# Probability-value products of an attention stage: FP32 against F32R in high and low parts

## The chip, the cores and the metric

The kernel runs on one core of a Trainium2 chip. The metric is the device time of one execution in microseconds, lower is better. The times shown are the median of the runs named; the profile is one further execution.

## The reference

A two-layer trunk over 512 latent tokens of width 1024, with 256 context tokens. Layer 0 mixes with a gated DeltaNet (4 heads) and, beside it, grouped attention; layer 1 mixes with a short convolution; both have a gated MLP. The change touches the attention alone:

```python
def gqa_softmax(q, k, v):
    # q: (B, Tq, 8 heads, 64); k, v: (B, S, 2 heads, 64)
    qg = q.reshape(b, tq, ATT_KV_HEADS, ATT_GROUPS, ATT_HD)
    s = jnp.einsum('bqkgd,bskd->bkgqs', qg, k) * (ATT_HD ** -0.5)
    p = jax.nn.softmax(s, axis=-1)
    o = jnp.einsum('bkgqs,bskd->bqkgd', p, v)
```

Queries are the 512 latent tokens, keys and values all 768 tokens. Everything is FP32.

## The kernel before, in words

All tensors lie with features or tokens over the 128 partitions. The heavy products (input and output projections, MLP) hold every operand as an F32R high part and a low part (the value less its high part) and make three F32R products of each pair: high by high, high by low, low by high. ScalarE writes high parts of weights (`split_hi`, line 1386), VectorE low parts (`split_lo`, line 1781). Each engine has its own program, written out in order; semaphores tie them, and an engine that waits holds up all that stands behind in its program.

The attention follows the DeltaNet. Two query heads, one for each key head, are worked as a pair p (4 pairs), one in partitions 0 to 63 and one in 64 to 127. A pair has 6 key tiles n of 128 keys; g = 6 p + n counts 24 items. Three things are done:

- Row maxima of a pair: `row_fill` (line 946, TensorE) makes scores of 128 queries by 384 keys for both heads into banks 2 and 3, and `row_max` (line 2080, VectorE) reduces each bank. The next `row_fill` waits for that reduction, as there is one pair of banks. A pair needs 8 of these. The first pair's stand before item 0; those of pair p + 1 are done in items n = 0 to 3 of pair p, two an item, so 12 of the 24 items have them. `row_peak` joins them and POOL writes them as a diagonal (`peak_diag`, line 2612), which a product with ones takes off the scores.
- Scores, keys over partitions: `scores_turned(g)` (line 970) makes eight matmuls into two banks, 0 and 1 or 4 and 5 by turns. It waits for the exponential of item g - 2 (semaphore `pexp`). ScalarE takes the exponential of the 128x1024 scores into `prob` (line 1588).
- Values: `values(g, half)` (line 990) multiplies `V1[half]` (64 columns of values, 64 of ones, so that the sums come along) by the probabilities of one head, in FP32, and adds over n in banks 6 and 7. It is issued two items behind the scores (`VALUE_LAG`), first half between the two row fills, second half behind them.

The TensorE loop (line 1107) has also columns of the modulation vectors (`mod_part`), `head_sums` in items 12 to 15 (each waits for a square that ScalarE issues at the end of its item), `sums_turned` and `inverse_rows` at n = 4 and 5, and `head_rows` in items 18 to 21. In item 16 the columns wait for a square root (`osd`, line 1629).

ScalarE's loop (line 1615) has, per item, the exponential, half of a modulation product (`mod_products`, four scalings of 128x256, items 0 to 21), and at some items `heads_out` (four copies that free banks 6 and 7; items 7, 13, 19), `head_hi` (12, 18), squares (11 to 14) and high parts of DeltaNet heads (19 to 22). POOL adds up each modulation product in three additions (line 2486) after every second item. VectorE's loop (line 2252) has the row maxima, `inverse_sums` and `heads_normed` at n = 4 and 5, `gated` (18 to 21) and `gated_lo` (20 to 23). When the last `gated_lo` is done (`mix0`), ScalarE makes the high part of the first weights of the output projection (line 1635), VectorE the low part, and `out_units` (line 1210) begins.

V comes in as `av`, is turned by TensorE (`value_turns`), and copied by ScalarE from PSUM into `V1` (line 1579), beside the last DeltaNet step. VectorE then makes the last six row-maximum pairs of pair 0 (line 2213).

## Time and profile before

| | us |
|---|---|
| median of 3 runs | 1664.26 (1662.99 to 1668.65) |
| the profiled execution | 1658.18 |
| its span, first to last instruction | 1656.4 |
| TensorE busy | 1550.1 (94%) |
| VectorE busy | 838.1 (51%) |
| ScalarE busy | 648.6 (39%) |
| POOL busy | 306.0 (18%) |

The profiled execution was 6 us faster than the median of the runs, and 5 faster than the fastest; its durations are used against its own time. Matmuls overlap, so the distance from one start to the next says more than a duration. PEclk is the granted TensorE clock as a share of 2.4 GHz; 0.50 is 1.2 GHz.

### The profile page before, as it was taken

Reading aid. Unit: us, or ns where it says so; the run is one execution under the profiler, and the core shown is the slowest. Engines: PE = TensorE matmul, PEld = TensorE weight load, DVE = VectorE, ACT = ScalarE, POOL = GpSimd, SP = SyncE. Lnnn points to the kernel's source line nnn. Section 1 sums busy time; section 2 is a strip of 40 time slices with the busy share of each in tenths; the row PEclk is TensorE's granted clock in tenths of the full one; section 3 lists DMA queues with packets and bytes.
Section 4 is the critical chain, followed back from the end, with each engine's and each line's share of the span. In section 5 each row is a group of like instructions: output and inputs, shape, how many; then the busy total and the mean of one; then the engine's idle time right before and its main releaser. Section 6 shows DMA issues by size and latency. Waiting matters only on the chain.

```text
span 1656.4 us, 19507 instructions
## 1 busy us (share of the span) xinstructions
PE 1550.1 (94%) x7832; PEld 1251.0 (76%) x7832; DVE 838.1 (51%) x1119; ACT 648.6 (39%) x990; POOL 306.0 (18%) x218
## 2 busy tenths in 40 slices
PE   8899896689979999899999999899998999999997
PEld 2688686578964557688888888778886888888886
DVE  2645523886553237755544343566667544444222
ACT  2443446301225564255533222256542434443221
POOL 3028602334644443000000011000021000000000
PEclk9999899679989999999999999899999999999999
DMA  9325601000021215134423222255522233222221
GB/s 349 102 89 175 181 26 39 1 1 1 1 77 62 92 51 153 51 118 137 131 96 101 92 93 96 93 163 184 170 86 67 76 102 101 83 95 96 92 93 51
DMA packets 153908, 160.19 MB, mean 97 GB/s; under 512 B 11383, under 2 KB 151144, under 8 KB 152808
## 3 DMA queue, kind: packets, MB, share of 16 engines
q1 hardware_dynamic: 153344, 158.95, 29.9%
q8 instruction: 53, 0.87, 0.2%
q10 hardware_dynamic: 488, 0.18, 0.0%
q14 instruction: 23, 0.19, 0.0%
HBM read 157.03 MB, written 2.10 MB: 96 GB/s over the span
## 4 chain that ended last, share of the span: by engine, by line
PE 82%; DVE 10%; ACT 2%; POOL 2%; issue 2%; DMA 0%; SPq 0%; DVEq 0%; ACTq 0%; POOLq 0%
PE ps L600 19%; PE ps L602 19%; PE ps L601 19%; PE ps L998 2%; PE ps L960 2%; DVE sub_prod L1996 1%; DVE blocks_inv L1999 1%; PE ps L985 1%; PE ps L1148 1%; PE ps L658 1%; PE ps L1150 1%; PE ps L1149 1%; DVE w_lo L1781 1%; PE ps L1170 1%; DVE att_top L2085 1%
## 5 line engine op out<-in xcount | busy, mean ns | idle before, releaser
L1781 DVE TENSOR_TENSOR w_lo<-w_raw,w_hi 128x2048 fp32r<-128x2048 f32 x100 | 234.2, 2342 | 454.0 <-ACT w_hi L1386 454.0
L600 PE MATMUL ps<-h_hi,w_hi 128*128 128x512 f32 x968 | 378.5, 391 | 2.0 <-DVE w_lo L1781 2.0
L601 PE MATMUL ps<-h_lo,w_hi 128*128 128x512 f32 x968 | 377.5, 390 | 0.0
L602 PE MATMUL ps<-h_hi,w_lo 128*128 128x512 f32 x968 | 377.4, 390 | 0.0
L1386 ACT ACTIVATE w_hi<-w_raw 128x2048 fp32r<-128x2048 f32 x100 | 191.3, 1913 | 258.9 <-PE ps L602 222.4
L600 PEld LDWEIGHTS ps<-h_hi,w_hi 128*128 128x128 f32 x968 | 182.2, 188 | 40.2 <-DVE w_lo L1781 2.6
L602 PEld LDWEIGHTS ps<-h_hi,w_lo 128*128 128x128 f32 x968 | 182.2, 188 | 38.1
L601 PEld LDWEIGHTS ps<-h_lo,w_hi 128*128 128x128 f32 x968 | 182.3, 188 | 37.6
L2635 POOL TENSOR_TENSOR sum_acc_y<-sum_acc_y,sum_y 128x512 f32<-128x512 f32 x18 | 25.7, 1427 | 584.1 <-ACT sum_y L1655 584.1
L600 PE MATMUL ps<-mid_hi,w_hi 128*128 128x512 f32 x338 | 133.0, 394 | 0.0
L602 PE MATMUL ps<-mid_hi,w_lo 128*128 128x512 f32 x338 | 131.8, 390 | 0.0
L601 PE MATMUL ps<-mid_lo,w_hi 128*128 128x512 f32 x338 | 131.5, 389 | 0.0
L2635 POOL TENSOR_TENSOR tmp<-tmp,tmp 128x512 f32<-128x512 f32 x6 | 7.8, 1295 | 379.1 <-ACT tmp L1651 379.1
L602 PEld LDWEIGHTS ps<-mid_hi,w_lo 128*128 128x128 f32 x338 | 63.4, 188 | 13.4
L601 PEld LDWEIGHTS ps<-mid_lo,w_hi 128*128 128x128 f32 x338 | 63.5, 188 | 12.9
L600 PEld LDWEIGHTS ps<-mid_hi,w_hi 128*128 128x128 f32 x338 | 63.5, 188 | 12.8
L2486 POOL TENSOR_TENSOR mod_raw_e<-mod_raw_e 128x1024 f32<-128x1024 f32 (+1 forms) x24 | 57.4, 2392 | 84.6 <-ACT mod_raw_e L1440 83.7
L2085 DVE TENSOR_REDUCE att_top<-ps 128x1 f32<-128x384 f32 x64 | 32.7, 552 | 58.3 <-PE ps L960 58.1
L2486 POOL TENSOR_TENSOR mod_raw_c<-mod_raw_c 128x1024 f32<-128x1024 f32 (+2 forms) x33 | 49.1, 1487 | 44.3 <-ACT mod_raw_c L1597 42.6
L2288 DVE TENSOR_SCALAR y<-ps,post_w 128x512 f32<-128x512 f32 x32 | 23.9, 748 | 63.8 <-ACT tmp L1651 30.3
L1703 ACT ACTIVATE mid_hi<-tmp 128x512 f32 (+1 forms) x44 | 27.1, 633 | 66.4 <-DVE tmp L2392 66.4
L998 PE MATMUL ps<-prob,V 128*128 128x512 f32 x96 | 52.7, 647 | 0.1
(374 smaller groups left out, 2611.3 us busy)
## 6 DMA issues: line engine op xcount, KB each, us to landing
w_raw<-in_ffn_w_up SPq DMA_DIRECT2D x44, 1024.0 KB, 5.1
w_raw<-in_ffn_w_down SPq DMA_DIRECT2D x16, 896.0 KB, 4.8
mod_raw_e<-in_mod_w SPq DMA_DIRECT2D x12, 1024.0 KB, 5.3
w_raw<-in_sc_w_in SPq DMA_DIRECT2D x12, 1024.0 KB, 5.3
mod_raw_c<-in_mod_w SPq DMA_DIRECT2D x11, 1024.0 KB, 5.2
mod_raw_s<-in_mod_w SPq DMA_DIRECT2D x11, 1024.0 KB, 7.9
w_raw<-in_hyb_w_in SPq DMA_DIRECT2D x9, 1024.0 KB, 7.9
mod_raw_a<-in_mod_w SPq DMA_DIRECT2D x8, 1024.0 KB, 16.1
```

Source lines behind the costliest of these rows:

```text
L600: mm(dst, hi, xh[:, k0 + k, :], start=first and k == 0, stop=False)
L601: mm(dst, hi, xl[:, k0 + k, :], start=False, stop=False)
L602: i = mm(dst, lo, xh[:, k0 + k, :], start=False, stop=last and k == nk - 1)
L960: m = mm(bank(2 + half, 384), q[r, p, qs], k[r, ks], start=i == 0, stop=i == 2)
L998: mm(bank(6 + half), V1[half][:, n, :], prob[g % 4][:, half * SEQ:(half + 1) * SEQ], start=n == 0, stop=n == NT - 1).then_inc(sem("pv"), 1)
L1386: nc.scalar.activation(whi[s][:, :], raw[s][:, :], ACT.Copy).then_inc(sem("w_hi"), 1)
L1703: nc.scalar.activation(mid_hi[:, bass.ds(2 * i + (2 * j0 + r), 1), :].rearrange("p c t -> p (c t)"), tmp[2 * par + r][:, :], ACT.Copy).the ...
L1781: V.tensor_tensor(wlo[s][:, :], raw[s][:, :], f32(whi[s][:, :]), ALU.subtract).then_inc(sem("w_lo"), 1)
L2085: V.tensor_reduce(top[:, c:c + 1], bank(2 + half, 384), AX.X, ALU.max).then_inc(sem("mx"), 1)
L2288: V.tensor_scalar(y[:, t, :], b, pw, None, ALU.mult).then_inc(sem("yev"), 1)
L2486: G.tensor_tensor(dst, a, b, ALU.add).then_inc(sem("mod_acc"), 1)
L2635: G.tensor_tensor(a[:, :], a[:, :], q[t % 2][:, :], ALU.add).then_inc(sem("ya"), 1)
```

## The change

`V1` and `prob` become F32R high parts (`Vh`, `PTh`) and low parts (`Vl`, `PTl`). ScalarE takes the exponential of an item twice, once into the F32R high part and once in FP32 into one of two `prob` buffers (now where `tmp` lies); VectorE subtracts the first from the second (`probability_lo`), one item behind, between the two `row_max` of an item. `values` makes three F32R products for one FP32 product and waits for the low part. `scores_turned` waits for both exponentials. Ahead of the loop VectorE writes the low part of V, in front of six pairs of row maxima, and POOL sets the other halves.

```diff
@@ -178,9 +178,12 @@
         peak = region("att_peak", 2 * 8, 107.125)
         isum = region("att_isum", 8, 107.1875)
         one_r = region("one_r", P, 107.5, F32R)
-        prob = [region(f"prob{i}", 2 * SEQ, 62 + 4 * i) for i in range(4)]
+        PTh = [region(f"PTh{i}", 2 * SEQ, 62 + 4 * i, F32R) for i in range(4)]
+        PTl = [region(f"PTl{i}", 2 * SEQ, a0, F32R) for i, a0 in enumerate((78, 82, 108, 112))]
+        prob = [place(f"prob{i}", 2 * SEQ, F32, tmp_at + 4 * K * i) for i in range(2)]
         diag = [region(f"peak_diag{i}", 2 * SEQ, 40 + 4 * i, F32R) for i in range(2)]
-        V1 = [view(region(f"V1{i}", NT * P, 116 + 3 * i), "p (n t) -> p n t", t=P) for i in range(2)]
+        Vh = [view(region(f"Vh{i}", NT * P, a0, F32R), "p (n t) -> p n t", t=P) for i, a0 in enumerate((116, 122))]
+        Vl = [view(region(f"Vl{i}", NT * P, a0, F32R), "p (n t) -> p n t", t=P) for i, a0 in enumerate((119, 54))]
         att_o = region("att_o", SEQ, 48)
         att_s = region("att_s", SEQ, 50)
         att_n = region("att_n", SEQ, 52)
@@ -972,11 +975,11 @@
                 p, n = divmod(g, NT)
                 b = 4 * (g % 2)
                 if g == 0:
-                    pe.wait_ge(sem("V"), 3)
+                    pe.wait_ge(sem("V"), 5)
                     pe.wait_ge(sem("oe"), 8)
                     pe.wait_ge(sem("vset"), 1)
                 if g >= 2:
-                    pe.wait_ge(sem("pexp"), g - 1)
+                    pe.wait_ge(sem("pexp"), 2 * (g - 1))
                 if n == 0:
                     pe.wait_ge(sem("dg"), p + 1)
                 ks = slice(n * P, (n + 1) * P)
@@ -990,13 +993,15 @@
             def values(g, half):
 
                 p, n = divmod(g, NT)
-                pe.wait_ge(sem("pexp"), g + 1)
+                pe.wait_ge(sem("PT"), g + 1)
                 if g == 0:
-                    pe.wait_ge(sem("vset"), 3)
+                    pe.wait_ge(sem("vset"), 5)
                 if n == 0 and p:
                     pe.wait_ge(sem("ov"), 4 * (p - 1) + 2 * half + 2)
-                mm(bank(6 + half), V1[half][:, n, :], prob[g % 4][:, half * SEQ:(half + 1) * SEQ], start=n == 0,
-                   stop=n == NT - 1).then_inc(sem("pv"), 1)
+                b, cols = bank(6 + half), slice(half * SEQ, (half + 1) * SEQ)
+                mm(b, Vh[half][:, n, :], PTh[g % 4][:, cols], start=n == 0, stop=False)
+                mm(b, Vh[half][:, n, :], PTl[g % 4][:, cols], start=False, stop=False)
+                mm(b, Vl[half][:, n, :], PTh[g % 4][:, cols], start=False, stop=n == NT - 1).then_inc(sem("pv"), 1)
 
             def sums_turned(p):
 
@@ -1218,7 +1223,7 @@
                         if j:
                             pe.wait_ge(sem("scb"), KC - 2)
                         else:
-                            pe.wait_ge(sem("pexp"), NITEM)
+                            pe.wait_ge(sem("pexp"), 2 * NITEM)
                         for k in range(KC):
                             if j == 0 and k == 3:
                                 sums_turned(3)
@@ -1576,7 +1581,7 @@
             act.wait_ge(sem("V"), 1)
             act.wait_ge(sem("rp"), 2 * NT)
             for half, r in enumerate(HALF):
-                nc.scalar.activation(V1[half][:, :, r], bank(0, ALL).rearrange("p (n t) -> p n t", t=P)[:, :, r],
+                nc.scalar.activation(Vh[half][:, :, r], bank(0, ALL).rearrange("p (n t) -> p n t", t=P)[:, :, r],
                                      ACT.Copy).then_inc(sem("V"), 1)
             act.wait_ge(sem("oe"), 8)
 
@@ -1585,8 +1590,11 @@
                 act.wait_ge(sem("st"), g + 1)
                 if g >= 4:
                     act.wait_ge(sem("pv"), 2 * (g - 3))
-                nc.scalar.activation(prob[g % 4][:, :], bank(4 * (g % 2), 2 * SEQ), ACT.Exp,
-                                     scale=HD ** -0.5).then_inc(sem("pexp"), 1)
+                b = bank(4 * (g % 2), 2 * SEQ)
+                nc.scalar.activation(PTh[g % 4][:, :], b, ACT.Exp, scale=HD ** -0.5).then_inc(sem("pexp"), 1)
+                if g >= 2:
+                    act.wait_ge(sem("PT"), g - 1)
+                nc.scalar.activation(prob[g % 2][:, :], b, ACT.Exp, scale=HD ** -0.5).then_inc(sem("pexp"), 1)
 
             def mod_products(j, half):
 
@@ -2210,10 +2218,22 @@
                     dve.wait_ge(sem("mod_done"), 2 * SC0)
                 V.tensor_tensor(sums_tile(j), t[:, 0, :], t[:, 1, :], ALU.add).then_inc(sem("late"), 1)
 
+            dve.wait_ge(sem("Sp"), 2 * NT - 2)
+            for half, r in enumerate(HALF):
+                dve.wait_ge(sem("V"), 3)
+                V.tensor_tensor(Vl[half][:, :, r], bank(0, ALL).rearrange("p (n t) -> p n t", t=P)[:, :, r],
+                                f32(Vh[half])[:, :, r], ALU.subtract).then_inc(sem("V"), 1)
             for j in range(2, NL):
                 for f in range(2):
                     row_max(0, j, f)
             row_peak(0)
+
+            def probability_lo(g):
+
+                dve.wait_ge(sem("pexp"), 2 * (g + 1))
+                if g >= 4:
+                    dve.wait_ge(sem("pv"), 2 * (g - 3))
+                V.tensor_tensor(PTl[g % 4][:, :], prob[g % 2][:, :], f32(PTh[g % 4][:, :]), ALU.subtract).then_inc(sem("PT"), 1)
 
             def inverse_sums(p):
 
@@ -2254,6 +2274,8 @@
                 fills = p + 1 < NPAIR and n < 4
                 if fills:
                     row_max(p + 1, n, 0)
+                if g:
+                    probability_lo(g - 1)
                 if g in (12, 18):
                     heads_lo(p - 2)
                 if fills:
@@ -2271,6 +2293,7 @@
                     gated(g - 18)
                 if 20 <= g:
                     gated_lo(g - 20)
+            probability_lo(NITEM - 1)
             dve.wait_ge(sem("mod_done"), 2 * (ATT0 + 8))
             split_lo(U_WOUT, 0)
             heads_lo(2)
@@ -2607,7 +2630,8 @@
             pool.wait_ge(sem("Sp"), 2 * NT - 2)
             for half in range(2):
                 r = HALF[1 - half]
-                G.memset(V1[half][:, :, r], 1.0).then_inc(sem("vset"), 1)
+                G.memset(f32(Vh[half])[:, :, r], 1.0).then_inc(sem("vset"), 1)
+                G.memset(f32(Vl[half])[:, :, r], 0.0).then_inc(sem("vset"), 1)
 
             def peak_diag(p):
 
```

## Rows read from the trace of the kernel before

**Rows 1.** Page, part 1: busy us, share of the span, instructions.

```profile
PE 1550.1 (94%) x7832; PEld 1251.0 (76%) x7832; DVE 838.1 (51%) x1119; ACT 648.6 (39%) x990; POOL 306.0 (18%) x218
```

**Rows 2.** Page, part 4: chain of waits, shares of the span by line.

```profile
PE ps L600 19%; PE ps L602 19%; PE ps L601 19%; PE ps L998 2%; PE ps L960 2%; DVE sub_prod L1996 1%; DVE blocks_inv L1999 1%; PE ps L985 1%; PE ps L1148 1%; PE ps L658 1%; PE ps L1150 1%; PE ps L1149 1%; DVE w_lo L1781 1%; PE ps L1170 1%; DVE att_top L2085 1%
```

**Rows 3.** Windows: us, busy of PE, PEld, DVE, ACT, POOL; PEclk, DMA, GB/s.

```profile
505.00:520.00 15.00, 14.69 (x65) 6.97 (x62) 4.25 (x9) 8.43 (x17) 8.24 (x7) 1.00 0.17 52
...
580.00:595.00 15.00, 12.02 (x51) 7.03 (x52) 1.08 (x4) 7.00 (x13) 5.42 (x4) 0.77 0.21 70
```

**Rows 4.** Timeline of PE, items 3 to 5: start, us, [idle before, releaser].

```profile
510.46 1.13 PE L998 MATMUL ps<-prob,V 128*128 128x512 f32 x2
511.74 0.44 PE L960 MATMUL ps<-ak_hi,aq_hi 64*128 64x384 f32 x2 [0.16 <-DVE att_top L2085]
...
517.25 0.50 PE L985 MATMUL ps<-aq_hi,ak_hi 64*128 64x512 f32 x2
...
518.72 1.88 PE L998 MATMUL ps<-prob,V 128*128 128x512 f32 x4
520.52 0.50 PE L985 MATMUL ps<-aq_hi,ak_hi 64*128 64x512 f32 x2
```

**Rows 5.** Timeline of ACT, item 4.

```profile
515.20 1.02 ACT L1588 ACTIVATE prob<-ps 128x1024 f32<-128x1024 f32 x1 [2.74 <-PE ps L987]
516.12 1.69 ACT L1597 ACTIVATE mod_raw_c<-mod_raw_c,cvec 128x256 f32<-128x256 f32 x4
```

**Rows 6.** Timeline of PE, output projection, first and last of 31 starts.

```profile
638.00 0.39 PE L600 MATMUL ps<-mix_hi,w_hi 128*128 128x512 f32 x1
...
644.80 0.39 PE L600 MATMUL ps<-mix_hi,w_hi 128*128 128x512 f32 x1
```

**Rows 7.** Timeline of PE, item 14.

```profile
565.70 1.02 PE L1031 MATMUL ps<-const,o_square 128*128 128x1 f32 x8 [0.35 <-ACT o_square L1625]
```

**Rows 8.** Timeline of PE and ACT, item 16.

```profile
581.31 1.28 ACT L1629 ACT_TABLE_LOAD   x1
...
582.98 0.56 PE L620 MATMUL ps<-const,mod_raw_c 128*128 128x1 f32 x2 [4.32 <-issue]
...
583.39 2.05 PE L998 MATMUL ps<-prob,V 128*128 128x512 f32 x2
...
585.24 0.42 PE L620 MATMUL ps<-const,mod_raw_c 128*128 128x1 f32 x2
```

**Rows 9.** Timeline ahead of item 0: ACT, DVE, POOL.

```profile
477.06 0.85 ACT L1579 ACTIVATE V<-ps 128x384 f32<-128x384 f32 x2
...
480.99 0.69 DVE L2061 TENSOR_TENSOR oT<-oT,ps 128x512 f32<-128x512 f32 x1 [1.15 <-PE ps L927]
...
489.01 1.90 POOL L2620 TENSOR_TENSOR peak_diag<-const,att_peak 128x1024 fp32r<-128x1024 f32 x1 [6.98 <-DVE att_peak L2093]
```

**Rows 10.** Groups of VectorE instructions: busy us, mean ns, idle before.

```profile
L2085 DVE TENSOR_REDUCE att_top<-ps 128x1 f32<-128x384 f32 x50 | 25.5, 552 | 54.3 <-PE ps L960 54.2
...
L2205 DVE TENSOR_TENSOR mod_raw_f<-mod_raw_f 128x1024 f32<-128x1024 f32 x6 | 7.3, 1214 | 0.0
```

**Rows 11.** Timeline of POOL and DVE, item 20.

```profile
601.60 4.86 POOL L2486 TENSOR_TENSOR mod_raw_c<-mod_raw_c 128x1024 f32<-128x1024 f32 x3 [3.92 <-ACT mod_raw_c L1597]
...
601.85 2.67 DVE L2244 TENSOR_TENSOR oT<-oT,gT 128x512 f32<-128x512 f32 x1
```

**Rows 12.** Timeline of PE and ACT, item 18 to the output projection.

```profile
593.09 0.50 PE L985 MATMUL ps<-aq_hi,ak_hi 64*128 64x512 f32 x2
...
618.95 1.91 ACT L1386 ACTIVATE w_hi<-w_raw 128x2048 fp32r<-128x2048 f32 x1 [3.05 <-DVE mix_lo L2249]
...
623.30 0.50 PE L1231 MATMUL ps<-mix_hi,w_hi 128*128 128x512 f32 x1 [1.65 <-DVE w_lo L1781]
```

**Rows 13.** Windows of PE: us, PE busy, PEclk, DMA, GB/s.

```profile
486.00:489.00 3.00, 1.07 (x6) 0.66 0.87 276
...
621.00:624.00 3.00, 1.35 (x5) 1.00 0.28 75
```

## The prediction

> **What bounds the kernel now.** I read the page first: TensorE is busy 94% of the span, VectorE 51%, ScalarE 39% [rows 1]. In the chain of waits the weight products (lines 600 to 602) hold over half; the probability-value product, line 998, the line to be changed, holds 2% [rows 2]. So what can move lies in the attention stage, from about 491 to 623 us. The windows show TensorE full there (14.8 of 15 us) and ScalarE at little more than half; only 580 to 595 has a hole and a low granted clock [rows 3].
>
> Then the TensorE timeline of single items. There are 24 items g (head pair p, key tile n). In an item without row maxima, line 998 takes 518.72 to 520.52, 1.80 us for two FP32 products (two records each), and the pitch is 3.27 us. In an item with row maxima (12 of them, 10 with values) each half of the values stands alone, and the second row product waits for VectorE's two reductions of the first: the values after 510.46 end before that wait (0.16 us) does [rows 4].
>
> ScalarE takes 0.92 us from one start to the next for the exponential and 1.60 for four scalings (1.70 less the same overlap of 0.1), 2.52 an item [rows 5].
>
> **TensorE.** 48 FP32 products become 144 F32R ones. F32R products of this shape in the output projection start 31 times in 6.80 us, 0.227 apart [rows 6]. Three are 0.68 against 0.86 for one FP32 product (1.80 less 0.08 for the change of tile shape, halved): 0.17 saved per half, 0.35 per item, 8.3 us over 24 items if all of it shows. It doesn't:
> - Items 2, 3, 6 to 9, 12, 14, 15: the first half's saving falls into the wait for VectorE [rows 4]; 9 x 0.17 = 1.5.
> - Items 4, 5, 10: all, 3 x 0.35 = 1.0. ScalarE's new 3.44 us is above their pitch, but they come in pairs after items with slack (ScalarE was idle for 2.74 us before item 4's exponential [rows 5]) and TensorE runs two items ahead.
> - Item 11 leads to head_sums, which wait for a square that ScalarE issues behind exponentials and scalings. One more exponential (0.92) eats the slack: 0. Item 13: head_sums already waited 0.35 for that square [rows 7]. There ScalarE's waits for values go and the exponential comes, and the square is ready when it was: 0.
> - Item 17: 0.35.
> Together -2.9.
>
> **Item 16.** TensorE stands 4.32 us while ScalarE does exponential, scalings, a table load and a square root [rows 8]. The second exponential lies in that chain: +0.92. The item's values then run at the low clock ([rows 3]: a mean of 0.77 over 15 us is 1.2 GHz for 6.9 of them), where one FP32 product and its column took 1.85 [rows 8]; three F32R products at twice 0.227 are 1.36, so about 0.35 of its 1.72 is saved per half, 0.7. Net +0.2.
>
> **The start.** V's low part is two VectorE subtractions of 128x384 from PSUM, behind the last oT addition (481.68) and ahead of the row maxima on which the first diagonal, and so all items, wait [rows 9]. Nearest rows: 0.69 for 128x512 from PSUM, 0.55 for a 128x384 reduction [rows 9, 10]. I take 0.52 each, +1.1 (bounds 0.9 and 1.4). V's high copies are done by 477.9 and hide. POOL's extra memsets hide in its 6.98 us of idle time before the diagonal [rows 9]. No DMA is added; SP's loads of modulation weights follow the columns, which stay behind their additions as now.
>
> **VectorE's low part.** 24 subtractions of 128x1024 in SBUF. The same shape elsewhere takes 1.21 us [rows 10]. In an item with maxima it stands between the two pairs of reductions: from the end of the first row product 0.1 + 1.0 + 1.2 + 1.0 = 3.4 us (with issue), and the next row product is due after 1.3 + 0.7 + 0.8 + 1.6 = 4.4. It costs nothing while that 1 us of cover holds; values run two items late, so they don't wait.
> But two-input VectorE work in SBUF does wait for POOL. At 601.85 a 128x512 product took 2.67 us instead of 0.69, until POOL's 128x1024 addition from 601.60 was over [rows 11]. POOL adds after every second item. In the maxima items its last, shortest addition meets the subtraction: up to 0.9 us late, just covered. Should it be the longest (2.3), 1.4 us would show, in three items (7 to 8 and the like): bound +4, I take 0.
>
> **The last six items** (18 to 23, no maxima). I drew up a schedule from 593.09 (t = 0) with the durations above, queue by queue. ScalarE: 1.84 + 1.60 for items 18 to 21, 1.84 for the others, 2.2 for heads_out, 0.5 for each of five high parts, first start at 1.7, end near 24.0. That alone would hold the loop some 1 us longer than now. VectorE: item 18's gated ends at 8.0, the low part of item 18 at 9.2, gated(1) waits for POOL's first addition until 12.1, the low part of item 19 for the second until 14.6; TensorE needs it at 12.9. The low part of item 21 lands at 23.6 (wanted at 21.6), so inverse_rows(2), heads_normed(2) and gated_lo(3) end at 28.9; w_hi, which waits for the last of them, now starts at 25.9. Behind it stand w_hi (1.9) and w_lo (the rest of the 4.35 us to the projection), then the output projection: 33.2 against 30.2 [rows 12]. So this stretch, instead of giving 6 x 0.35 = 2.1, costs +3.0. Bounds: +1 if VectorE always gets in ahead of POOL (ScalarE alone), +5 if every low part meets an addition.
>
> **Sum:** -2.9 + 0.2 + 1.1 + 3.0 = **+1.4 us**. The profiled execution took 1658.18 (span 1656.4) and would become 1659.6. The median of the runs shown is 6 us above it, so the forecast is 1664.3 + 1.4 = **1665.7**. Elsewhere nothing changes: the probability buffers move to free places, F32R outputs cost ScalarE no more (w_hi's 128x2048 takes 1.91 [rows 12]).
>
> **Rivals.**
> *A. The clock falls (slower).* In the schedule TensorE waits 1.8 us in item 21, 2 in item 23, 1.5 in the two value rounds behind it and 2 before the output projection. In this trace the granted clock fell between 486 and 489, where TensorE waited for row maxima and was busy 1.07 of 3 us; yet from 621 to 624 it was busy 1.35 of 3 and kept 1.00 [rows 13]. It decides if the waits from item 21 on are as dense as those ahead of 487. The Trainium skill, TensorE: Matmul & The Clock Gate, HAM oscillation, says that matmul bursts with waits between keep losing the full clock; by that rule this change, which puts waits between short bursts, would lose it here, while the rows speak both ways. Price: the low stretch of item 16 lasted 6.9 us [rows 3]; once or twice that at 1.2 GHz costs the output projection 3.5 to 7. With the +1.4 and the upper bound of the late stretch: +5 to +10, 1669 to 1674. Chance 0.2.
> *B. Everything is covered (faster).* VectorE beats POOL, ScalarE's idle time absorbs the exponentials (it works 8.4 of 15 us [rows 3]), and the last items give their 2.1. Then -2.9 - 2.1 + 0.2 + 1.1 = -3.7, 1660.6; with the whole 8.3 saved and the start free it is -8.3 + 0.9 = -7.4, 1657. For it: the average idle. Against: the last items' queues. Chance 0.12 for somewhere under 1662, 0.06 for over 0.3%.
> *C. The maxima items become bound by VectorE.* Up to 1.4 us in three items, and a little in others: +4 on top, 1669 to 1670. Chance 0.1.
> *D. It saves TensorE nothing.* If the three products came 0.29 us apart they would take the 0.86 of the FP32 one: 0 + 0.9 + 1.1 + 3.0 = +5.0, 1669.3. Against it: the 31 starts of the same shape and type [rows 6]. Chance 0.02.
>
> **Numbers.** Forecast 0.56, within 1662 to 1669. A change under 0.3% (5 us) can't be told from none. Slower by more: most of A and a little of C, 0.18. Faster: 0.06. Same: 0.76. The range takes in B's partial case below and A's above: 1659.5 to 1672.
>
> **What would show it.** Line 998's successors 0.227 us apart in threes; the first row product after them waiting about 0.3 instead of 0.16; the two VectorE subtractions before the third pair of reductions, diagonal 1 us later; the hole at item 16 at 5.2 us; low parts of 1.2 us, some of 2 to 3.5 where POOL adds; TensorE waiting in items 21 and 23 for them; w_hi of the output projection issued some 3 us later after the start of item 18. Wrong if the maxima items lengthen (then C), if the last six items shrink (B), or if the granted clock in the output projection is below 1 (A).

## The result, and the profile after

The changed kernel took 1673.59 us (median of 6 runs, 1670.40 to 1683.72), the kernel before 1667.47 in the same comparison (6 runs, 1662.99 to 1672.90): ratio 1.0066, interval 1.0043 to 1.0088. A second comparison, ten runs of the changed kernel beside 33 of before, gave 1.0062 (1.0036 to 1.0088). The medians alone are 6.1 us apart in the first comparison and 11.8 in the second (1678.04 against 1666.21). So it is slower by some 10 us; the forecast of no change was wrong, and 1673.59 is above the range. Of the 7.9 us between it and the forecast of 1665.7, 3.2 are the kernel before itself, whose median was 1664.26 when the forecast was made and 1667.47 here.

The profiled execution took 1672.36 (span 1670.6), 14.2 more than that of before. The page's part 1 for the kernel after:

```profile
PE 1557.5 (93%) x7880; PEld 1270.1 (76%) x7880; DVE 870.8 (52%) x1145; ACT 669.3 (40%) x1014; POOL 315.6 (19%) x220
```

TensorE is busy 7.4 us more than in [rows 1], though its products were to take 8.3 less. I cut both traces at landmarks: the end of the last oT addition, and the starts of the first score product of some items (line 985 before, 988 after). In us:

| stretch | before | after | difference | predicted |
|---|---|---|---|---|
| start to the last oT addition | 481.68 | 485.51 | +3.8 | 0 |
| to item 0 | 9.37 | 11.33 | +1.96 | +1.1 |
| items 0, 1 | 11.87 | 12.66 | +0.79 | 0 |
| items 2 to 15 | 74.11 | 79.22 | +5.11 | -2.5 |
| item 16 | 11.33 | 11.39 | +0.06 | +0.2 |
| item 17 | 4.73 | 4.02 | -0.71 | -0.35 |
| item 18 to the output projection | 30.21 | 31.85 | +1.64 | +3.0 |
| projection to the end | 1033.10 | 1034.62 | +1.5 | 0 |

The first and last rows hold code that the change does not touch; the clock that an execution happens to get moves them, which I call its draw: between 250 and 480 us the windows add up to 68 us below full clock here and 58 before, and 58 again in the second profiled execution of the changed kernel (its start takes 482.04). That leaves 8.9 us between the last oT addition and the projection, where I had +1.4, and 5.11 of it where I had a gain.

The reason stands in the windows of TensorE in items 6, 14 and 23 of the kernel after (columns: us, PE busy, PEclk, DMA share, GB/s):

```profile
528.00:531.00 3.00, 2.10 (x14) 1.00 0.00 0
531.00:534.00 3.00, 2.78 (x13) 0.67 0.18 44
534.00:537.00 3.00, 3.00 (x10) 0.50 0.91 306
...
573.00:576.00 3.00, 2.54 (x17) 1.00 0.00 0
576.00:579.00 3.00, 3.00 (x14) 0.57 0.02 5
...
633.00:636.00 3.00, 1.45 (x7) 1.00 0.08 15
```

A PEclk of 0.50 is 1.2 GHz. The clock fell twice amid busy work, at about 532 and 576, and came back some seven us later each time; in the kernel before it is 1.00 from 501 to 582. Products at 1.2 GHz take nearly twice as long (timeline, item 6): their starts are 0.42 apart, where they are 0.23 apart at 2.4 GHz.

```profile
533.97 0.63 PE L1003 MATMUL ps<-PTl,Vh 128*128 128x512 f32 x1
534.39 0.63 PE L1004 MATMUL ps<-PTh,Vl 128*128 128x512 f32 x1
```

Between 480 and 660 us the windows of the kernel after add up to 44.4 us at 1.2 GHz, before to 20.5. The difference is the two stretches in the items and a longer one at the start: 23.9 us, from 487.7 to 511.6, against 13.7 before. The longer one reaches 2.1 us into item 2, which takes 6.00 where the second profiled execution has 5.12; so 0.9 of the +5.11 comes from the start and not from the items' own waits. In the last window, where Rival A looked for the fall, TensorE waits half of the time and keeps 1.00.

What TensorE does ahead of such a fall, item 3 of the kernel after (timeline):

```profile
517.77 0.50 PE L1002 MATMUL ps<-PTh,Vh 128*128 128x512 f32 x1
518.11 0.39 PE L1003 MATMUL ps<-PTl,Vh 128*128 128x512 f32 x1
518.34 0.40 PE L1004 MATMUL ps<-PTh,Vl 128*128 128x512 f32 x1
519.05 0.45 PE L963 MATMUL ps<-ak_hi,aq_hi 64*128 64x384 f32 x2 [0.32 <-DVE att_top L2093]
```

Here the three products are 0.23 apart, as forecast, and the wait behind them is 0.32 instead of 0.16 [rows 4], as forecast too. Item 6 has a longer one (timelines of POOL, VectorE and TensorE, kernel after):

```profile
521.25 2.81 POOL L2644 TENSOR_TENSOR peak_diag<-const,att_peak 128x1024 fp32r<-128x1024 f32 x1 [7.14 <-DVE att_peak L2101]
...
524.03 10.79 POOL L2509 TENSOR_TENSOR mod_raw_c<-mod_raw_c 128x1024 f32<-128x1024 f32 x6
...
524.33 3.18 DVE L2236 TENSOR_TENSOR PTl<-prob,PTh 128x1024 fp32r<-128x1024 f32 x1 [2.02 <-ACT prob L1597]
...
529.60 0.35 PE L623 MATMUL ps<-const,mod_raw_c 128*128 128x1 f32 x2 [0.90 <-POOL mod_raw_c L2509]
```

POOL's diagonal takes 2.81 instead of 1.90 [rows 9], its additions run late, VectorE's low part takes 3.18 instead of 1.21 [rows 10], and the column product of item 6 waits 0.90 us for POOL. VectorE and POOL delay each other.

### The profile page after: what moved, and what is told of

Its sections match the earlier page's. It is cut to its first block, busy times and chain, and to the rows that moved or that the text cites. A ratio compares the mean times of both kernels' runs of the same rounds, so it can differ in the third digit from the quotient of the medians.

```text
span 1670.6 us, 19676 instructions
## 1 busy us (share of the span) xinstructions
PE 1557.5 (93%) x7880; PEld 1270.1 (76%) x7880; DVE 870.8 (52%) x1145; ACT 669.3 (40%) x1014; POOL 315.6 (19%) x220
## 4 chain that ended last, share of the span: by engine, by line
PE 77%; DVE 11%; POOL 4%; ACT 4%; issue 3%; DMA 0%; SPq 0%; DVEq 0%; ACTq 0%; POOLq 0%
PE ps L603 18%; PE ps L605 18%; PE ps L604 18%; POOL mod_raw_e L2509 2%; PE ps L963 2%; DVE blocks_inv L2007 2%; DVE sub_prod L2004 1%; PE ps L1153 1%; PE ps L661 1%; DVE w_lo L1789 1%; PE ps L1154 1%; PE ps L1155 1%; PE ps L1175 1%; PE ps L988 1%; PE ps L719 1%
## 5 line engine op out<-in xcount | busy, mean ns | idle before, releaser
L603 PEld LDWEIGHTS ps<-mid_hi,w_hi 128*128 128x128 f32 x338 | 63.9, 189 | 12.7
L2509 POOL TENSOR_TENSOR mod_raw_c<-mod_raw_c 128x1024 f32<-128x1024 f32 (+2 forms) x33 | 54.9, 1663 | 42.9 <-ACT mod_raw_c L1605 41.1
L1704 ACT ACTIVATE tmp<-tmp 128x512 f32<-128x512 f32 x44 | 27.8, 633 | 62.8 <-DVE tmp L2397 62.2
```

The source lines that it names most:

```text
L603: mm(dst, hi, xh[:, k0 + k, :], start=first and k == 0, stop=False)
L1704: nc.scalar.activation(tmp[2 * par + r][:, :], tmp[2 * par + r][:, :], ACT.Silu).then_inc(sem("sg"), 1)
L2509: G.tensor_tensor(dst, a, b, ALU.add).then_inc(sem("mod_acc"), 1)
```

## Experiments

Two theories after the result. Theory C: the shorter products leave TensorE more waiting in the maxima items, and the clock falls there. Theory Q: the added work in the queues of ScalarE, VectorE and POOL costs the time. A third is that the low clock at the start carries over into the items.

**No low part at all.** One exponential, no subtraction; the second product reads PTh, so three F32R products remain.

```diff
-                pe.wait_ge(sem("PT"), g + 1)
+                pe.wait_ge(sem("pexp"), 2 * (g + 1))
...
-                mm(b, Vh[half][:, n, :], PTl[g % 4][:, cols], start=False, stop=False)
+                mm(b, Vh[half][:, n, :], PTh[g % 4][:, cols], start=False, stop=False)
...
-                nc.scalar.activation(PTh[g % 4][:, :], b, ACT.Exp, scale=HD ** -0.5).then_inc(sem("pexp"), 1)
-                if g >= 2:
-                    act.wait_ge(sem("PT"), g - 1)
-                nc.scalar.activation(prob[g % 2][:, :], b, ACT.Exp, scale=HD ** -0.5).then_inc(sem("pexp"), 1)
+                nc.scalar.activation(PTh[g % 4][:, :], b, ACT.Exp, scale=HD ** -0.5).then_inc(sem("pexp"), 2)
...
-                if g:
-                    probability_lo(g - 1)
...
-            probability_lo(NITEM - 1)
```

> The changed kernel without the second exponential and without VectorE's low part of the probabilities; the second of the three F32R products takes the high part again, so TensorE does the same work and the low part of the probabilities is left out of the result. Theory Q (the loss comes from the queues: ScalarE's second exponential, VectorE's subtraction and its waits for POOL): all of it goes, TensorE saves its 0.35 us an item where no row maxima bind, and the kernel comes out 3 to 6 us under the kernel before, a ratio of 0.997. Theory C (the loss is granted clock: two extra stretches at 1.2 GHz in items 6 and 14, because short waits of TensorE follow shorter products): waits for row maxima are still 0.3 us per maxima item, stretches at 1.2 GHz stay between 512 and 588 us, and the time is within 3 us of the kernel before or above it.

Measured: 1663.60 (10 runs), ratio 0.9988 (0.9964 to 1.0013). Items 2 to 15 take 74.71, with low clock in the first 2.0 us of item 2 and from 575 to 582; item 16 takes 10.54 and the last stretch 28.76. From 1.0062 and 1.0066 to 0.9988 is some 12 us: so much hangs on the second exponential and the subtractions, with what they do to the clock. And the F32R products alone bring nothing that can be measured over the whole kernel.

**FP32 product, all the rest kept.** One FP32 product of PTh and Vh, both FP32; both exponentials, all subtractions and their waits stay (the regions `PTh` and `Vh` are declared FP32 too).

```diff
-                mm(b, Vh[half][:, n, :], PTh[g % 4][:, cols], start=n == 0, stop=False)
-                mm(b, Vh[half][:, n, :], PTl[g % 4][:, cols], start=False, stop=False)
-                mm(b, Vl[half][:, n, :], PTh[g % 4][:, cols], start=False, stop=n == NT - 1).then_inc(sem("pv"), 1)
+                mm(b, Vh[half][:, n, :], PTh[g % 4][:, cols], start=n == 0, stop=n == NT - 1).then_inc(sem("pv"), 1)
```

> The changed kernel with all that ScalarE, VectorE and POOL do, but with one FP32 product of the high parts (kept in FP32 here) as in the kernel before: only TensorE's part is undone. The low parts are computed and not used. Theory Q: the queues cost what they cost and TensorE saves nothing, so it is as slow as the changed kernel or up to 3 us slower, 8 to 14 us above the kernel before. Theory C: TensorE's waits in maxima items shrink to those of the kernel before, the granted clock stays at 1.00 from 512 to 588 us, and the kernel is 3 to 6 us above the kernel before: 2 of the start, 3 of the last items, 1 of item 16.

Measured: 1672.43, ratio 1.0037 (1.0014 to 1.0060). The clock stays up in items 2 to 15 (windows of TensorE, the kernel with the FP32 product):

```profile
531.00:534.00 3.00, 2.94 (x16) 1.00 0.04 9
534.00:537.00 3.00, 3.00 (x17) 1.00 1.01 328
...
576.00:579.00 3.00, 2.94 (x14) 1.00 0.07 22
```

They take 75.55, 1.4 more than before. But the low clock of the start reaches 2.2 us into item 2 here as well (6.23 against 5.27), so the queue work itself costs 0.5 in items 3 to 15 (69.32 against 68.85). It costs 0.8 in item 16 (12.15) and 1.7 in the last stretch (31.89). Ahead of item 2 this execution is 2.7 longer, with 23.9 us of low clock at the start against 13.7; how much of that is the queue's was not told apart. So both halves of the cause count: the queue work by itself, and the low clock in the items, which is absent here with the longer product.

**Filler in the maxima items.** One extra 128x512 F32R product of 0.23 us, its result never read, behind the first half of the values in each of the ten maxima items that have values.

```diff
+                if fills and g >= VALUE_LAG:
+                    pe.wait_ge(sem("pexp"), 2 * g)
+                    mm(bank(4 * ((g + 1) % 2)), Vh[0][:, n, :], PTh[(g - VALUE_LAG) % 4][:, 0:SEQ], start=True, stop=True)
```

> The changed kernel with one extra F32R 128x512 product (0.23 us, result overwritten) in each of ten items with row maxima, where TensorE waits 0.31 us for VectorE. Theory C: TensorE is busy through these waits, fewer stretches at 1.2 GHz between 512 and 588 us, 3 to 7 us faster than the changed kernel. Theory Q: the waits for the queues are what they were, the filler is hidden or costs 0.1 an item: same time to 1 us slower.

Measured: 1667.76, ratio 1.0022 (1.0004 to 1.0040). Windows of TensorE in this kernel:

```profile
549.00:552.00 3.00, 2.73 (x27) 1.00 0.07 21
552.00:555.00 3.00, 3.00 (x21) 1.00 0.00 0
555.00:558.00 3.00, 3.00 (x18) 1.00 0.49 137
558.00:561.00 3.00, 3.00 (x20) 1.00 0.61 213
...
570.00:573.00 3.00, 3.00 (x23) 1.00 0.94 315
...
585.00:588.00 3.00, 3.00 (x12) 0.50 0.59 182
```

Items 2 to 15 take 72.97 instead of 79.22, with no low clock until item 16's hole. More work made the items shorter by 6 us, of which 0.9 is item 2, where this execution has no low clock from the start (73.22 to 67.85 for items 3 to 15). TensorE waits for no reduction there any more. The filler is F32R too, so the type of the products alone does not bring the clock down; the gaps between them are what was changed.

**V's low part later**, behind the row maxima and the peak of pair 0.

```diff
             dve.wait_ge(sem("Sp"), 2 * NT - 2)
+            for j in range(2, NL):
+                for f in range(2):
+                    row_max(0, j, f)
+            row_peak(0)
             for half, r in enumerate(HALF):
...
-            for j in range(2, NL):
-                for f in range(2):
-                    row_max(0, j, f)
-            row_peak(0)
```

> The changed kernel with V's low part written by VectorE behind the row peak of pair 0 instead of ahead of the last six pairs of row maxima. Both theories: the 1.0 us leaves the chain to the first scores (11.3 us from the end of the last oT addition in the changed kernel, 9.4 in the kernel before), so 10.3 or less. Theory C adds that the extra low-clock row products ahead of the diagonal go too, 9.4 to 9.6, 2 us in all; theory Q gives 1.0.

Measured: 1667.41, ratio 1.0036 (1.0011 to 1.0062). Item 0 starts 10.20 behind the last oT addition instead of 11.33: the 1.1 is the two subtractions, which the timeline of the changed kernel has as one row:

```profile
485.42 1.01 DVE L2224 TENSOR_TENSOR Vl<-ps,Vh 128x384 fp32r<-128x384 f32 x2
```

In total it can't be told from the changed kernel; its trace too has a low stretch inside the items (531 to 538).

**Second exponential without the subtraction.** As in the first experiment, but ScalarE keeps both exponentials, the second never read and without its wait for PT.

> The changed kernel with ScalarE's second exponential but without VectorE's low part of the probabilities (the second product takes the high part again, the low part is left out of the result). It splits the cost of the last six items, from the first scores of item 18 to the output projection: 31.9 us in the changed kernel, 28.8 without both, 30.2 before. If ScalarE's serial work holds them, 30.5 to 31.9; if VectorE's waits for POOL hold them, 28.8 to 29.5. Item 16 (to the first scores of 17) should stay at 11.4 and be 10.5 only without the exponential. Whole kernel: 0 to 3 us above the kernel before.

Measured: 1663.46, ratio 0.9987 (0.9961 to 1.0013). Last stretch 29.74, between the two answers that I had allowed; items 2 to 15 72.71, with 3.4 us of low clock from 574; item 16 11.39, as expected.

**Subtraction without the second exponential.** PTl is PTh minus PTh, of the same shape.

```diff
-                V.tensor_tensor(PTl[g % 4][:, :], prob[g % 2][:, :], f32(PTh[g % 4][:, :]), ALU.subtract).then_inc(sem("PT"), 1)
+                V.tensor_tensor(PTl[g % 4][:, :], f32(PTh[g % 4][:, :]), f32(PTh[g % 4][:, :]), ALU.subtract).then_inc(sem("PT"), 1)
```

> The changed kernel with VectorE's subtraction of the same size, but of the high part from itself, and without the second exponential (the low part is zero, left out of the result). If VectorE behind POOL holds the last six items, they take 31 to 31.9 us here; if ScalarE does, 28.8 to 29.5. Item 16 takes 10.5. The column product of item 6, for which TensorE waited 0.9 us on POOL's additions, waits here too if VectorE's subtractions are what delays POOL. Whole kernel: 0 to 3 us above the kernel before.

Measured: 1669.13, ratio 1.0017 (0.9991 to 1.0044). Items 2 to 15 take 79.69, with low clock until 511 (5.2 us of item 2) and from 573 to 586; item 16 takes 10.83, with low clock from 590; the last stretch takes 32.96, of which part is 3 us of low clock at 624. The column product of item 6 waits 1.09 us for POOL, as it does with the real subtraction, and 0.23, for VectorE, without any: so the subtractions are what delays POOL. The exponential costs 1 us in the last stretch (28.76 to 29.74) and 0.5 in item 12 (6.40 to 6.90); the subtraction is the expensive one of the two.

**The changed kernel again.**

> The changed kernel again, beside the others on one chip. Theory C (granted clock): it is the slowest of the four, 7 to 12 us above the kernel before, and its profile has at least one stretch at 1.2 GHz between 512 and 588 us. If the first comparison owed its size to where the clock happened to fall, 4 to 7 us. Theory Q has no reason for a change from run to run.

Measured: 1678.04 (10 runs, 1670.21 to 1683.33), ratio 1.0062 (1.0036 to 1.0088). Its profiled execution has one long stretch at 1.2 GHz in place of two short ones (windows of TensorE):

```profile
552.00:555.00 3.00, 2.73 (x20) 1.00 0.00 0
555.00:558.00 3.00, 2.78 (x12) 0.58 0.17 45
558.00:561.00 3.00, 3.00 (x10) 0.50 0.89 304
...
600.00:603.00 3.00, 3.00 (x13) 0.50 0.75 228
603.00:606.00 3.00, 3.00 (x22) 0.95 0.38 127
```

Low from 555 to 603; items 2 to 15 take 85.66, item 16 12.56. The place of the fall differs from one execution to the next; the ten runs lie in two groups, 1670.2 to 1675.6 with a mean clock of 0.947 to 0.950, and 1680.5 to 1683.3 with 0.941 to 0.943. The six runs of the first comparison lie in the same two groups, four and two.

**All gaps filled.** Fillers as above, V's low part later, and the kernel's own `warm` products (line 1104 of the changed kernel) in three places: one before each of pair 0's last four row products, four ahead of item 0, five in item 16's hole. (The text on the kernel before speaks of six such pairs of row maxima; line 1104 and the trace have four.)

```diff
             for j in range(2, NL):
                 for f in range(2):
+                    warm(5, 1)
                     row_fill(0, j, f)
+            warm(5, 4)
...
+                if g == 16:
+                    pe.wait_ge(sem("pexp"), 32)
+                    warm(4, 5)
```

> The changed kernel with filler products in ten maxima items, V's low part behind the first row peak, and filler products (FP32, 0.86 us) between the last row products of pair 0, ahead of the first scores and in the hole of item 16. Theory C: no stretch at 1.2 GHz from 487 to 640 us; against the changed kernel that gives back 5 us in the maxima items, 3 to 4 at the start and 2 behind item 16, so 1 to 4 us under the kernel before. Theory Q: only the 1 us of V's low part, and the fillers cost up to 1: as slow as the changed kernel.

Measured: 1659.93 (12 runs, 1654.68 to 1661.99), ratio 0.9963 (0.9944 to 0.9982). That is 6 us under the kernel before, where 1 to 4 were expected. No low clock between 480 and 660 us. Windows of TensorE from item 6 to item 16:

```profile
519.00:534.00 15.00, 14.33 (x80) 1.00 0.23 72
534.00:549.00 15.00, 14.91 (x90) 1.00 0.44 139
549.00:564.00 15.00, 14.20 (x91) 1.00 0.22 71
564.00:579.00 15.00, 14.91 (x72) 1.00 0.22 71
```

**The kernel before, with the warm products at the start and in item 16 only** (the last edit; the count waited for is 16, since it has one exponential an item).

> The kernel before with the same FP32 fillers between the last row products of pair 0, ahead of the first scores and in the hole of item 16. Theory C: the stretches at 1.2 GHz at 487 and 582 us go, 20 us of low clock in all; the time from the last oT addition to the output projection falls from 141.6 to about 136 (start -1, items 0 and 1 -3.5, item 16 -2), and the kernel is 3 to 6 us under the kernel before, 0 to 3 above or under the changed kernel with all fillers. That says what the change itself is worth with the clock held: near nothing.

Measured: 1658.22 (12 runs, 1653.92 to 1665.33), ratio 0.9952 (0.9930 to 0.9975). That is 8 us under the kernel before, where 3 to 6 were expected. No low clock between 480 and 660 us either, and without a filler in the items. This pair shows the change with the clock held in both: from the last oT addition to the projection 136.57 with the F32R products, 135.79 without, a difference of 0.8. In the first kernel V's low part stands behind the row maxima; where the change has it, it costs 1.1 more, so with the clock held the change would cost about 1.9 (an estimate from these two differences), against the +1.4 of the forecast. Pitch from item to item (from the starts of the first score products):

```
item        2    3    4    5    6    7    8    9   10   11   12   13   14   15
before   5.27 5.34 3.73 3.28 5.67 5.34 5.67 5.35 4.17 4.29 6.57 6.13 7.16 6.13
changed  5.11 5.17 3.40 2.93 6.73 5.18 5.52 5.17 3.82 3.98 6.90 5.98 7.10 5.98
```

**Ends filled, items not.** The kernel with all gaps filled, less the ten fillers.

> The version with all fillers, less the ten of 0.23 us in the maxima items. Theory C: the clock starts full at 490 and falls in some executions and stretches between 512 and 588 us, where the waits of 0.3 us stand again; 3 to 8 us slower than with all fillers, near the kernel before, with runs further apart than those of the version with all fillers (7 us from lowest to highest). If the low clock of those items was only a consequence of the low start, it stays full and the time equals that with all fillers.

Measured: 1671.76 (12 runs, 1659.73 to 1672.62), ratio 1.0011 (0.9986 to 1.0035). The start is as full as in the last two kernels (item 0 at 10.15, items 0 and 1 in 8.33), and yet the clock falls in item 12. Timeline, then windows of TensorE, of this kernel:

```profile
552.66 1.02 PE L1036 MATMUL ps<-const,o_square 128*128 128x1 f32 x8 [0.26 <-ACT o_square L1638]
...
555.74 0.59 PE L623 MATMUL ps<-const,mod_raw_c 128*128 128x1 f32 x2 [0.22 <-DVE att_top L2098]
556.26 0.69 PE L963 MATMUL ps<-ak_hi,aq_hi 64*128 64x384 f32 x2
```

```profile
552.00:555.00 3.00, 2.74 (x20) 1.00 0.00 0
555.00:558.00 3.00, 2.78 (x12) 0.63 0.10 27
558.00:561.00 3.00, 3.00 (x10) 0.50 0.94 322
...
588.00:591.00 3.00, 3.00 (x9) 0.50 0.00 0
```

Two waits of a quarter of a microsecond, then 37.5 us at 1.2 GHz: items 2 to 15 take 85.63 instead of 72.97. The fall is no consequence of the low clock at the start; that rival is out, but for the 0.9 us of item 2. The fall is a matter of chance in part: two of the 12 runs took 1659.7, seven 1671.7 to 1672.6, which is about the 12.7 us that the profile shows. With all fillers none of 12 runs was above 1662.0, and none of ten above 1660.6 in the next version, which was timed on the same chip as this one.

**POOL's late additions cut.** The kernel with all gaps filled, but POOL's additions of the modulation products from 20 on are one column wide; most of that sum is left out.

```diff
-                mod_add(3 * j, slot[:, 0:4, :], slot[:, 0:4, :], slot[:, 4:8, :])
+                w = slice(0, 1) if 20 <= j < LATE else slice(0, UW)
+                mod_add(3 * j, slot[:, 0:4, w], slot[:, 0:4, w], slot[:, 4:8, w])
```

> The version with all fillers, with POOL's additions of the last three modulation products (those behind items 17, 19 and 21) cut to one column of 256; most of that sum is left out of the result. If VectorE's waits for POOL hold the last six items, they take 29.5 to 30.5 us from the first scores of item 18 to the output projection instead of 31.9, and VectorE's subtractions there take 1.2 us each. If the plain length of VectorE's and ScalarE's work holds them, 31.5 to 31.9.

Measured: 1658.29, ratio 0.9951 (0.9932 to 0.9970). Last stretch 29.72 instead of 31.86. The subtractions there, first in the kernel with all gaps filled, then in this one (timelines of VectorE, other rows left out):

```profile
602.96 1.22 DVE L2244 TENSOR_TENSOR PTl<-prob,PTh 128x1024 fp32r<-128x1024 f32 x1
...
606.08 3.42 DVE L2244 TENSOR_TENSOR PTl<-prob,PTh 128x1024 fp32r<-128x1024 f32 x1
...
611.11 1.74 DVE L2244 TENSOR_TENSOR PTl<-prob,PTh 128x1024 fp32r<-128x1024 f32 x1
```

```profile
605.45 1.22 DVE L2244 TENSOR_TENSOR PTl<-prob,PTh 128x1024 fp32r<-128x1024 f32 x1
608.82 1.22 DVE L2244 TENSOR_TENSOR PTl<-prob,PTh 128x1024 fp32r<-128x1024 f32 x1
612.13 1.23 DVE L2244 TENSOR_TENSOR PTl<-prob,PTh 128x1024 fp32r<-128x1024 f32 x1 [0.66 <-ACT prob L1605]
```

So 2.1 us of the last stretch are VectorE's waits for POOL, and the subtractions themselves are hidden there: without them, but with the second exponential, it took the same 29.74.

**All profiled executions together.** Low clock between the first scores of item 3 and of item 16, one execution each:

| version | us at 1.2 GHz |
|---|---|
| FP32 products: before; before with warm products; FP32 product in the changed kernel | 0, 0, 0 |
| F32R products, no fillers in the items: the changed kernel, twice; V's low part later; ends filled | 13.7, 33.8; 6.8; 33.7 |
| the same without subtractions: one exponential; two | 6.8; 3.4 |
| the same with the subtraction, one exponential | 13.0 |
| F32R products, fillers in the items: fillers alone; all gaps filled; POOL's late additions cut | 0, 0, 0 |

All seven with shorter products and open waits have it and none of the six others. The subtractions are not needed for a fall. The sizes are draws, as the two executions of the changed kernel show, and executions that were not profiled can differ.

## Why the prediction was wrong, by its steps

**The step that failed** is in the part on TensorE: "the first half's saving falls into the wait for VectorE; 9 x 0.17". I booked the saved time as a longer wait that costs nothing. The wait came to the size I gave it (0.32), but with such waits the clock of TensorE fell in all seven profiled executions, and at 1.2 GHz the products behind it take nearly twice as long (0.42 us against 0.23). I had set a price on a fall of the clock only behind item 21; in the maxima items it stood at nothing. In place of -2.5 for items 2 to 15 stand +5.1 in one profiled execution and +11.5 in the other (74.11 against 85.66). With the ten waits filled it is -1.1. The link from the waits to the clock rests on filling them: no fall in three profiled executions with the fillers, at least one in each of the seven without. Ten extra products in another place were not tried.

**Rival A** named this mechanism and put it in the wrong place: I looked for the long waits (items 21, 23 and the projection), and those kept the full clock, while short ones in a stretch that I read as "full" lost it. Its span, 1669 to 1674, holds the median by luck: it was worked out from late waits and the late stretch, which is not how the time came. The sign that I gave for Rival C, maxima items that lengthen, came true through the clock too. Behind the rows: the Trainium skill, TensorE: Matmul & The Clock Gate, A second HAM failure mode, describes a kernel in which TensorE idles briefly between groups of matmuls, often enough for the clock to swing. By that rule this would have been the rival to price; the trace agrees with it, with waits of 0.2 to 0.3 us ahead of the fall at 555.7. I had taken the section ahead of it, on longer waits.

**TensorE with the clock held.** The pitches of the two kernels without low clock give 0.15 to 0.18 for items 2, 3, 7, 8, 9 and 15 (forecast 0.17), 0.33 to 0.35 for 4, 5 and 10 (0.35), 0.31 for 11 and 0.15 for 13 (forecast 0 for both), 0.06 for 14 (forecast 0.17; its wait for the square grew from 0.35 to 0.45). Two items went the other way, where 0.17 was forecast: 6 by +1.06 and 12 by +0.33. Without the subtractions item 6 takes 5.51 and 5.53, with them and one exponential 6.84: it is VectorE's low parts that hold POOL up ahead of it, which is Rival C's contention seen from the other side. I had asked only how late POOL makes VectorE. Item 12's +0.33 is there with the second exponential alone (6.90; 6.40 with one), and TensorE waits 0.25 there for ScalarE's square, before not at all: it is the square for head_sums, which I had given to item 11. Sum: -1.1 for the forecast's -2.5. (In the prediction 0.86 less 0.68 is 0.18, and so 8.6 over 24 items, not 8.3; and its sum for VectorE in a maxima item is 3.3, not 3.4. Neither matters here.)

**The start.** The subtractions measured 1.01 us (forecast 1.04) and held item 0 up by 1.1, as moving them showed. The other 0.9 of the +1.96, and the 0.8 of items 0 and 1, lie in a stretch where row products run at 1.2 GHz; the forecast took that stretch as unchanged. The low clock began 5.3 us behind the last oT addition in the kernel before, 2.2 behind it in the changed kernel and 4.3 in the version with the second exponential alone, which has V's low part ahead too: there item 0 comes 10.61 behind, +1.24, close to the forecast. And in the second profiled execution of the changed kernel, whose low stretch lasted 13.7 us as before, items 0 and 1 took 10.03, 1.8 less than before. So the 0.8 of items 0 and 1 is the draw's; whether V's low part makes the early fall likelier stays open.

**Item 16.** The hole is 5.23 us, predicted 5.2:

```profile
595.58 0.56 PE L623 MATMUL ps<-const,mod_raw_c 128*128 128x1 f32 x2 [5.23 <-issue]
```

Predicted +0.2, measured +0.06. That the exponential makes it is shown: 10.54 without it, 11.39 with it alone, +0.85 for the +0.92 of the forecast; and the three products give 0.79 (11.33 to 10.54) for the forecast's 0.7. Item 17 gave 0.71 for 0.35; in the pair with the clock held it is 0.31 (4.29 to 3.98), and the rest is the low stretch of item 16, which before ended 1.0 us into item 17.

**The last six items.** Predicted +3.0 with bounds +1 and +5, measured +1.64. The runs split it: the three products give -1.45 (28.76 against 30.21), the second exponential costs +1.0 (29.74), the subtractions behind POOL +2.1 (31.86 against 29.72). I had +1 against the kernel before for ScalarE alone, where -0.5 was measured (29.74 against 30.21), and +2 for VectorE behind POOL, which was right. So the mechanism held and the term for ScalarE was 1.5 too high. The timelines of VectorE, TensorE and ScalarE in the kernel after, items 21 to 23:

```profile
623.61 3.41 DVE L2236 TENSOR_TENSOR PTl<-prob,PTh 128x1024 fp32r<-128x1024 f32 x1
...
627.07 0.50 PE L1002 MATMUL ps<-PTh,Vh 128*128 128x512 f32 x1 [0.96 <-DVE PTl L2236]
...
631.61 1.92 ACT L1391 ACTIVATE w_hi<-w_raw 128x2048 fp32r<-128x2048 f32 x1 [3.52 <-DVE mix_lo L2269]
```

The low part from 623.61 meets POOL and makes TensorE wait 0.96 for it, as forecast in kind. w_hi starts 27.5 behind item 18 (604.13), where 28.9 was forecast and before has 25.9 [rows 12].

**Rivals B, C and D.** B is out by the time. C's price, VectorE late for TensorE in the maxima items, did not show: the wait for the reductions is 0.32, no more. D is out: the three products take 0.69 us, and the items without maxima are 0.31 to 0.35 shorter with the clock held.

## What to carry to other kernels

A wait is not free because the engine would have waited anyway: where TensorE is nearly full, as here, shortening its products lengthens its waits, and the granted clock can fall for many microseconds (3 to 34 in items 3 to 15 of these traces). Read the granted clock of the stretch in which a saving turns into waiting, in several executions, and try a product that nobody reads before deciding what a faster form is worth. Price a VectorE instruction with two inputs in SBUF on both queues: how late it makes POOL, and POOL it.

## What the hardware showed that I had not expected

- Ten products of 0.23 us, 2.3 us of work in all, made items 3 to 15 shorter by 5.4 us (73.22 to 67.85) in one pair of profiled executions, 12.7 in another (80.52 to 67.85).
- By the busy time in the records the stretches with and without a fall hardly differ: 2.74 and 2.78 of 3 us around the fall above, 2.73 in a window of the kernel with fillers that stayed at 1.00. And item 6 of the kernel with all gaps filled has a wait of 0.98 us for POOL without a fall, where waits of 0.90 and 0.91 stood ahead of one in the changed kernel and with V's low part later. The records show that the clock fell and what TensorE waited for; what else decides it stays open.
- The kernel before loses clock as well, at the start and in item 16: eight and five warm products there, with nothing else changed, give 0.9952 (0.9930 to 0.9975), the lowest ratio of a version that computes all of the reference. The filled kernel with F32R products also beats the kernel before and the changed one, at 0.9963 (0.9944 to 0.9982), which can't be told from 0.9952; the gain is the clock's, not the products'.
- A subtraction of 128x1024 that takes 1.21 us took up to 3.42 beside POOL, and POOL's work took longer as well: 2.81 instead of 1.90 for the diagonal. With POOL's additions one column wide each late one took 1.22. The Trainium skill, SBUF — State Buffer, Who interferes with whom, says that a VectorE instruction with two inputs in SBUF contends with a GpSimd (POOL) instruction that reads SBUF, and that the port pair they share is an exclusive lock; these rows agree.
